# The causal mask of the first attention: fp32 mask products on TensorE, or an addition on VectorE with the row minimum

## The chip, the core and the metric

The kernel runs on one core of a Trainium2 chip. The metric is device time in microseconds (us): the median of several executions. The profile is of one execution, and its times are counted from the start of its span.

## What is computed

The program is two model blocks in a row. The first has 2 layers on 256 tokens of 1024 numbers, the second has 2 layers with a 32-expert layer each. The change touches the mixer of the first layer alone, an attention of 16 heads with keys of 64 + 32 numbers and values of 64:

```python
def mla_mixer(h, positions, w_a, q_norm, kv_norm, w_uq, w_ukv, w_o):
    ...
    q = (c_q @ w_uq).reshape(b, s_len, MLA_HEADS, MLA_NOPE + MLA_ROPE)
    q = jnp.concatenate([q[..., :MLA_NOPE], apply_rope(q[..., MLA_NOPE:], positions)], axis=-1)
    ...
    o = causal_block_attention(q, k, v, (MLA_NOPE + MLA_ROPE) ** -0.5)
    return o.reshape(b, s_len, MLA_HEADS * MLA_V) @ w_o

def causal_block_attention(q, k, v, scale, log_forget_cumsum=None):
    for b0 in range(0, s_len, Q_BLOCK):          # 256 tokens: two blocks of 128 queries
        b1 = b0 + Q_BLOCK
        logits = jnp.einsum('bqhd,bkhd->bhqk', q[:, b0:b1], k[:, :b1]).astype(jnp.float32) * scale
        causal = k_idx[None, :] <= q_idx[:, None]
        logits = jnp.where(causal, logits, NEG_INF)
        probs = jax.nn.softmax(logits, axis=-1).astype(v.dtype)
        outs.append(jnp.einsum('bhqk,bkhd->bqhd', probs, v[:, :b1]))
```

## The kernel before

Every engine has a program of its own, written out in order, and waits on semaphores. Nothing is scheduled by a planner: the order of the code is the order on the engine.

The attention is cut into 32 units, one for a head and a tile of 128 queries. Even units (tile 0) have 128 keys, odd units (tile 1) have 256; two units make a pair, one head. For unit u:

- PE, `scores(u)`: the fp32 product of queries and keys (line 924), then a second fp32 product, identity times the mask, added in the same bank (line 926). The trace has two MATMUL records for each fp32 product. Four banks hold the scores of four units, so that PE runs four units ahead.
- DVE, `row_max(u)`: the negative row maximum (TENSOR_REDUCE, line 2078), and its product with the scale 96^-0.5 (TENSOR_SCALAR on one column, line 2081).
- ACT: the exponential (line 1412) reads the bank, with the scale and that column as bias, writes the probabilities to SBUF and reads out their row sum (two records). `copy_probs(u)` (line 1403) copies the turned probabilities from PSUM to SBUF.
- PE, `turn_probs(u)`: one or two 128x128 transposes (line 951), which wait for the exponential; `values(u)`: one or two fp32 products of 64 columns (line 937), which wait for the copy. There are two banks for the turned probabilities and two for the outputs.
- DVE, `combine(u)`: the reciprocal of the row sum (line 2096), which waits for the exponential; `finish(u)`: the output divided by it, to `tokens_out` (line 2103).

In its loop over u, PE does scores(u+4), turn_probs(u), values(u-1); ACT does the exponential of u, then copy_probs(u-1); DVE does combine(u), row_max(u+4), finish(u-1). scores(u+4) waits until the exponential of u has read the bank. On DVE each instruction also waits for the end of the one before it (`v` in the code).

Ahead of the attention DVE copies the products of `g_uq` (the queries) out of PSUM, turns the last 32 numbers of each head by their angles, and PE transposes queries and keys (line 870). Behind it `close_block` transposes the output, splits it in two parts on DVE, and then lets POOL begin on the low parts of the weights (`port_free`). Weights come through a ring of four slots of 1 MB. When the first probabilities have been turned, POOL issues a transfer of 9 MB within DRAM (`rel_rows_repeated`, line 1766), which the second layer needs, and a row of gains (`broadcast_row`, line 1704), which the step behind the attention needs.

The same `attention` functions serve the second block's two-map attention (`kind="diff"`), which has no mask.

Of the kernel before, what the change touches and what calls it, by code (L numbers as in the profile page):

```python
# [11 lines left out]
ALU = mybir.AluOpType  # L12
# [3 lines left out]
P = 128  # L16
# [46 lines left out]
def constants():  # L63

    c = np.zeros((P, C_END), np.float32)
    i = np.arange(P)
    c[:, C_IDENT:C_IDENT + P] = np.eye(P)
    c[:, C_FLIP:C_FLIP + P] = np.eye(P)[::-1]
    col = np.arange(2 * P)
    c[:, C_CAUSAL:C_CAUSAL + 2 * P] = np.where(P + i[:, None] - col[None, :] >= 0, 0.0, NEG)  # L70
    qc = i % GRID_W
    start = np.clip(qc - NA_COLS // 2, 0, GRID_W - NA_COLS)
    kc = np.arange(GRID_W)
    ok = (kc[None] >= start[:, None]) & (kc[None] < start[:, None] + NA_COLS)
    c[:, C_NAMASK:C_NAMASK + GRID_W] = np.where(ok, 0.0, -NEG)
    c[:, C_UPPER:C_UPPER + P] = i[:, None] < i[None, :]
    half = 16
    inv = (np.float32(10000.0) ** (-np.arange(half, dtype=np.float32) / np.float32(half))).astype(np.float32)
    t = np.arange(SEQ)
    ar = (t // GRID_W).astype(np.float32)[:, None] * inv  # L80
    ac = (t % GRID_W).astype(np.float32)[:, None] * inv
    cos = np.cos(np.concatenate([ar, ar, ac, ac], 1)).astype(np.float32)
    sin = np.concatenate([-np.sin(ar), np.sin(ar), -np.sin(ac), np.sin(ac)], 1).astype(np.float32)
    for n in range(LT):
        c[:, C_COS + 64 * n:C_COS + 64 * n + 64] = cos[n * P:(n + 1) * P]
        c[:, C_SIN + 64 * n:C_SIN + 64 * n + 64] = sin[n * P:(n + 1) * P]
    c[:, C_INV:C_INV + half] = inv
    c[:, C_EIDX:C_EIDX + NE] = np.arange(NE)
    c[:, C_OIDX:C_OIDX + MAX_OVER] = np.arange(MAX_OVER)
    c[0, C_SEL:C_SEL + P] = 1.0  # L90
    c[1, C_SEL + P:C_SEL + 2 * P] = 1.0

    hot = np.zeros((64, DIL_G, BIAS_LEN), np.float32)
    exact = BUCKETS // 2
    for g, dil in enumerate(DILATION):
        for m in range(BIAS_LEN):
            dist = 2 * P - 1 - m
            if dist >= 0 and dist % dil == 0 and dist // dil <= SPAN:
                n = np.float32(max(dist, 1))
                large = exact + int(np.float32(np.log(n / np.float32(exact)) / np.float32(math.log(MAX_DIST / exact))  # L100
                                               * np.float32(BUCKETS - exact)))
                hot[dist if dist < exact else min(large, BUCKETS - 1), g, m] = 1.0
            else:
                hot[BUCKETS, g, m] = NEG
    return c, hot.reshape(64, DIL_G * BIAS_LEN)
# [31 lines left out]
def build_program(nc, I, out):  # L137
    ctx = ExitStack()
    with ctx:
# [281 lines left out]
            return ccol[:, c:c + 1]  # L421

        class Unit:
            def __init__(self, maps, n_keys, scale, values, width, dest, bias=None, kind="", head=0, tile=0):
                self.maps, self.n_keys, self.scale, self.values = maps, n_keys, scale, values
                self.width, self.dest, self.bias, self.kind, self.head, self.tile = width, dest, bias, kind, head, tile

        def mla_units():

# [4 lines left out]
            for h in range(MLA_H):  # L434
                for t in range(LT):
                    n = (t + 1) * P
                    maps = [[(0, n, qT[0:MLA_DK, h, t * P:(t + 1) * P], kT[0:MLA_DK, h, 0:n],
                              ident, causal[:, 2 * P - n:2 * P])]]
                    values = [kv[:, k, h, NOPE:NOPE + MLA_V] for k in range(t + 1)]
                    units.append(Unit(maps, n, MLA_DK ** -0.5, values, MLA_V,  # L440
                                      y_tile(t)[:, h * MLA_V:(h + 1) * MLA_V], head=h, tile=t))
            return place(units, True)

        N_PAIRS = DIL_H // 2
# [41 lines left out]
        def diff_units(layer):  # L486

            units = []
            for h in range(4):
                for t in range(all_tiles[layer]):  # L490
                    k0 = 0 if t < LT else LT * P
                    n = MAX_TILES * P - k0
                    maps = [[(m * BANK, n, qaT[64 * m:64 * m + 64, h, t * P:(t + 1) * P],
                              kaT[64 * m:64 * m + 64, h, k0:], None, None)] for m in range(2)]
                    values = [va[:, k, h, :] for k in range(k0 // P, MAX_TILES)]
                    units.append(Unit(maps, n, 1.0, values, P,
                                      ar(YA + t * 512, 512)[:, h * P:(h + 1) * P], kind="diff", head=h, tile=t))
            return place(units, False)

        def na_steps(layer):  # L500
# [197 lines left out]
        def _(pe):  # L698
# [212 lines left out]
            def attention(units):  # L911
# [5 lines left out]
                def scores(u):  # L917
                    unit = units[u]
                    if u >= n_held:
                        pe.wait_ge(exp_ready, base[s_ready.name] + u - n_held + 1)  # L920
                    for parts in unit.maps:
                        for col, n, q, k, turn, bias in parts:
                            dst = unit.scores[:, col:col + n]
                            last = nc.tensor.matmul(dst, q, k, start=True, stop=bias is None)
                            if bias is not None:
                                last = nc.tensor.matmul(dst, turn, bias, start=False, stop=True)
                    last.then_inc(s_ready, 1)
                    made.next(s_ready)

# [425 lines left out]
        def _(act):  # L1355
# [38 lines left out]
            def attention(units):  # L1394
# [10 lines left out]

                for u, unit in enumerate(units):
                    act.wait_ge(max_ready, base + u + 1)
                    if u >= held(units):
                        act.wait_ge(pT_ready, base + u - held(units) + 1)
                    for m in range(len(unit.maps)):  # L1410
                        c = stat(units, u, m)
                        last = nc.scalar.activation(unit.probs[:, m * BANK:m * BANK + unit.n_keys],
                                                    unit.scores[:, m * BANK:m * BANK + unit.n_keys], ACT.Exp,
                                                    bias=small[:, 64 + c:65 + c], scale=unit.scale,
                                                    accum_out=small[:, 80 + c:81 + c])
                    last.then_inc(exp_ready, 1)
                    if u >= 1:
# [512 lines left out]
        def _(dve):  # L1930
# [134 lines left out]
            def attention(units):  # L2065
                def row_max(u):
                    unit = units[u]
                    dve.wait_ge(s_ready, seen.next(s_ready))
                    if unit.kind == "diff":
# [1 line left out]
                        v(red(small[:, c:c + 2], unit.scores.rearrange("p (m k) -> p m k", m=2)[:, :, 0:unit.n_keys], X,  # L2071
                              ALU.max, negate=True), max_ready)
                        return
                    for m in range(len(unit.maps)):
                        c = 64 + stat(units, u, m)
                        last = m == len(unit.maps) - 1
                        scores = unit.scores[:, m * BANK:m * BANK + unit.n_keys]
                        v(red(small[:, c:c + 1], scores, X, ALU.max, negate=True),
                          max_ready if last and unit.scale == 1.0 else dve_step)
                        if unit.scale != 1.0:  # L2080
                            v(ts(small[:, c:c + 1], small[:, c:c + 1], unit.scale, None, ALU.mult), max_ready)

                def combine(u):

# [313 lines left out]
            for part in (c1, c2, c3):  # L2398
# [15 lines left out]
            norm_turn(LT, lambda t: ar(AROW + t * wide + MLA_QR, MLA_KVR),  # L2414
                      lambda g, t, n: XT[:, 2816:3328].rearrange("p (k t c) -> p k t c", k=2, t=LT)[:, 0:2, t, :],
                      2, gain=lambda t: V[:, V_KVN:V_KVN + 2])
            copy_product(g_uq, lambda n, t: ar(QROW + t * 1536 + n * BANK, BANK))

            for t in range(LT):
                sin = ang[:, t * 16:(t + 1) * 16]  # L2420
# [559 lines left out]
```

## Time and profile before

| | |
|---|---|
| median of 3 runs | 3340.39 us (3333.77 to 3341.43) |
| span of the profiled execution | 3333.3 us |
| PE busy | 2806.4 us (84%) |
| DVE busy | 1275.1 us (38%) |
| ACT busy | 877.4 us (26%) |
| POOL busy | 1089.3 us (33%) |
| attention of the first layer | 103.16 to 143.64 us, 40.5 us |

The page gives the profiled execution's span; what lies around it is not recorded, and the median of the runs is 7.1 us above this span. Busy shares are averages over stages that differ much: the two expert layers stream weights at up to 400 GB/s, while the stage of the change is small matrices on PE, DVE and ACT. So the stage is read by itself, 103 to 144 us. In a timeline row a start time, a duration, the engine, the line of the kernel, the operation, out<-in, and the count of merged instructions follow each other; in brackets stands the idle time before it and what ended it.

### The profile page before, as it was taken

The page shows a single profiled execution, that of the slowest core. Times are in us where ns is not written, and L with a number is a line of the kernel's source. Part 1 is how long each engine was busy: PE and PEld are TensorE (multiplying, and loading weights), DVE is VectorE, ACT ScalarE, POOL GpSimd, SP SyncE. Part 2 cuts the span into 40 slices and gives each one's busy share as a digit, 9 for nine tenths or more (in the row PEclk, how much of TensorE's full clock was granted, in tenths as well). Part 3 has the DMA queues.
Part 4 walks back from the last instruction along what each step waited for, and adds up shares of the span by engine and source line. Part 5 has one row for each costly group of instructions (what it writes and reads, how often), then busy time and mean ns, then how long its engine had stood idle before and what let it go on. Part 6 is the DMA issues. An engine that isn't in the chain of part 4 may idle for free.

```text
span 3333.3 us, 35642 instructions
## 1 busy us (share of the span) xinstructions
PE 2806.4 (84%) x13137; PEld 1834.4 (55%) x13137; DVE 1275.1 (38%) x2356; ACT 877.4 (26%) x1211; POOL 1089.3 (33%) x508
## 2 busy tenths in 40 slices
PE   6889879998998987889985988885797886988885
PEld 3767757777776775568762333332684772333331
DVE  4632144345225224753343322223427443322223
ACT  0433322235334212522221111112225331111111
POOL 0267746632874342224321000001363651000000
PEclk9989989999999998989987999998898997998998
DMA  5545488862554352622247999999241567999997
GB/s 159 171 150 176 158 296 291 288 223 70 166 173 152 139 164 98 216 89 91 101 152 277 390 401 399 399 398 357 76 139 49 179 234 289 391 396 397 396 398 288
DMA packets 218797, 781.17 MB, mean 234 GB/s; under 512 B 15092, under 2 KB 16290, under 8 KB 168752
## 3 DMA queue, kind: packets, MB, share of 16 engines
q1 hardware_dynamic: 189856, 669.61, 54.7%
q0 software_dynamic: 28816, 109.88, 9.9%
q8 instruction: 81, 1.33, 0.2%
q14 instruction: 44, 0.36, 0.0%
HBM read 750.36 MB, written 63.14 MB: 244 GB/s over the span
## 4 chain that ended last, share of the span: by engine, by line
PE 52%; DMA 22%; DVE 13%; SPq 6%; POOL 4%; ACT 2%; issue 2%; DVEq 0%; POOLq 0%; ACTq 0%
PE banks L737 11%; PE banks L738 10%; PE banks L742 10%; DMA weight_ring<-in_moe_w_down 4%; SPq L606 4%; PE banks L1131 4%; DMA arena<-in_moe_w_gate 3%; POOL weight_ring_r L1737 3%; DMA x_transposed<-in_moe_w_up 3%; DMA weight_ring<-in_moe_w_up 3%; DMA weights_high<-in_moe_w_gate 3%; PE banks L1154 2%; DMA tokens_out<-in_moe_w_down 2%; PE banks L820 2%; PE banks L870 2%
## 5 line engine op out<-in xcount | busy, mean ns | idle before, releaser
L1737 POOL TENSOR_TENSOR weight_ring_r<-weight_ring,weights_high_r 128x2048 fp32r<-128x2048 f32 x136 | 620.8, 4573 | 510.4 <-ACT weights_high_r L1387 419.8
L1387 ACT ACTIVATE weights_high_r<-weight_ring 128x2048 fp32r<-128x2048 f32 x136 | 257.5, 1901 | 736.4 <-PE banks L742 325.3
L737 PE MATMUL banks<-weights_high_r,x_transposed_r 128*128 128x512 f32 x1008 | 401.2, 398 | 33.9 <-ACT weights_high_r L1387 9.9
L1882 POOL DMA_DIRECT2D moe_y<-arena x64 | 33.9, 530 | 938.1 <-DVE arena L2570 922.1
L742 PE MATMUL banks<-weight_ring_r,x_transposed_r 128*128 128x512 f32 x1328 | 325.2, 391 | 2.1 <-POOL weight_ring_r L1737 2.1
L1737 POOL TENSOR_TENSOR weight_ring_r<-weight_ring,gates_r 128x2048 fp32r<-128x2048 f32 (+1 forms) x60 | 270.8, 4523 | 135.0 <-ACT gates_r L1387 73.8
L742 PEld LDWEIGHTS banks<-weight_ring_r,x_transposed_r 128*128 128x128 f32 x1328 | 249.5, 188 | 57.2 <-POOL weight_ring_r L1737 5.5
L737 PEld LDWEIGHTS banks<-weights_high_r,x_transposed_r 128*128 128x128 f32 x1008 | 192.6, 191 | 88.5 <-issue 26.4
L1593 ACT ACTIVATE arena<-banks 64x1024 f32<-64x1024 f32 x64 | 65.4, 1021 | 598.0 <-PE banks L1131 598.0
L738 PE MATMUL banks<-weights_high_r,arena_r 128*128 128x512 f32 x520 | 205.7, 396 | 0.0
L2552 DVE TENSOR_TENSOR arena<-banks,arena 64x1024 f32<-64x1024 f32 x64 | 77.9, 1217 | 312.9 <-ACT arena L1593 312.9
L1154 PE MATMUL banks<-weight_ring,arena 128*64 128x512 f32 x496 | 139.2, 703 | 35.5 <-DMA weight_ring<-in_moe_w_down 32.0
L2570 DVE TENSOR_TENSOR arena<-banks,arena 64x1024 f32<-64x1024 f32 x64 | 77.9, 1217 | 218.2 <-ACT arena L1607 218.2
L1101 PEld LDWEIGHTS banks<-constants,arena 64*128 64x128 f32 x256 | 69.6, 318 | 156.6 <-issue 155.0
L738 PE MATMUL banks<-weights_high_r,tokens_out_r 128*128 128x512 f32 x384 | 152.8, 398 | 0.0
L1387 ACT ACTIVATE gates_r<-weight_ring 128x2048 fp32r<-128x2048 f32 (+1 forms) x60 | 112.2, 1883 | 147.8 <-DMA weight_ring<-in_dil_w_qkv 87.9
L870 PE MATMUL banks<-constants,scaled_rows 128*128 128x128 f32 x482 | 80.4, 322 | 78.4 <-DVE scaled_rows L2008 67.1
L1131 PE MATMUL banks<-weight_ring,arena 128*64 128x512 f32 x528 | 126.2, 600 | 22.6 <-DMA weight_ring<-in_moe_w_up 12.0
L1131 PE MATMUL banks<-arena 128*64 128x512 f32 x512 | 123.1, 603 | 11.7 <-DMA arena<-in_moe_w_gate 11.7
L1101 PE MATMUL banks<-constants,arena 64*128 64x64 f32 x256 | 87.2, 421 | 54.0 <-DMA arena<-moe_x 54.0
L738 PE MATMUL banks<-weights_high_r,x_transposed_r 128*128 128x512 f32 x336 | 132.3, 394 | 0.0
L1607 ACT ACTIVATE arena<-banks 64x1024 f32<-64x1024 f32 x64 | 65.4, 1021 | 246.4 <-PE banks L1154 246.4
(383 smaller groups left out, 4886.3 us busy)
## 6 DMA issues: line engine op xcount, KB each, us to landing
weight_ring<-in_moe_w_down SPq DMA_DIRECT2D x62, 1024.0 KB, 30.6
weight_ring<-in_w_in SPq DMA_DIRECT2D x56, 1024.0 KB, 5.2
weight_ring<-in_w_ada SPq DMA_DIRECT2D x48, 1024.0 KB, 7.3
weight_ring<-in_ffn_w_in SPq DMA_DIRECT2D x44, 1024.0 KB, 5.1
weight_ring<-in_dil_w_qkv SPq DMA_DIRECT2D x36, 1024.0 KB, 5.2
tokens_out<-in_moe_w_gate SPq DMA_DIRECT2D x34, 1024.0 KB, 29.8
arena<-in_moe_w_up SPq DMA_DIRECT2D x34, 1024.0 KB, 29.2
weight_ring<-in_moe_w_up SPq DMA_DIRECT2D x34, 1024.0 KB, 28.9
```

Source lines behind the costliest of these rows:

```text
L606: sp.dma_start(slot(c, KG, BANK), src[e, half]).then_inc(w_in[slots[c]], 16)
L737: nc.tensor.matmul(banks[t][:, 0:width], xh, wh[:, k, :], start=k0 + k == 0, stop=False)
L738: nc.tensor.matmul(banks[t][:, 0:width], xl, wh[:, k, :], start=False, stop=False)
L742: last = nc.tensor.matmul(banks[t][:, 0:width], lhs(k0 + k, t)[0], wl[:, k, :], start=False, stop=k0 + k == g.k_tiles - 1)
L870: last = nc.tensor.transpose(bank[0:m, n * P:(n + 1) * P], src, ident)
L1101: return nc.tensor.matmul(dst, src, ident[0:CAP, 0:CAP], start=True, stop=True)
L1131: last = nc.tensor.matmul(halves(ps[m], kt), x, w[:, k, :], start=kt < 2, stop=kt >= KD - 2)
L1154: last = nc.tensor.matmul(halves(ps[2 + n], k), h, w[:, k % 2, n * BANK:(n + 1) * BANK], start=half == 0, stop=half == 1)
L1387: nc.scalar.activation(high(s, kn, width), slot(c, kn, width), ACT.Copy).then_inc(high_ready, 1)
L1737: nc.gpsimd.tensor_tensor(slot(c, kn, width, ring_r), slot(c, kn, width), high(s, kn, width), ALU.subtract).then_inc(low_ready, 1)
L2552: tt(A[0:CAP, E_SUM:E_SUM + 2 * BANK], pair[0][0:CAP, :], A[0:CAP, E_UP:E_UP + 2 * BANK], ALU.add).then_inc(summed, 1)
L2570: tt(A[0:CAP, E_Y + par * D:E_Y + (par + 1) * D], pair[1][0:CAP, :], A[0:CAP, E_YR:E_YR + D], ALU.add).then_inc(y_ready, 1)
```

## The change

The mask's products go. The scores alone are made on PE. DVE reads them and the mask in one instruction (`tensor_tensor_reduce`), writes their sum to the place of the probabilities in SBUF, and leaves the minimum of each row. To make the minimum serve, the queries are multiplied with -96^-0.5 when DVE takes them out of PSUM, and the mask has +1e30 in place of -1e30; the exponential is then taken of minus the sum. The one-column product with the scale goes too. The exponential reads SBUF and writes over what it read, so that PE's scores(u+4) waits for the row minimum of u and no longer for its exponential; in return the row minimum of u+4 waits until the probabilities of u have been turned, since it writes where they lie, and the exponential needs no such wait any more.

```diff
-    c[:, C_CAUSAL:C_CAUSAL + 2 * P] = np.where(P + i[:, None] - col[None, :] >= 0, 0.0, NEG)
+    c[:, C_CAUSAL:C_CAUSAL + 2 * P] = np.where(P + i[:, None] - col[None, :] >= 0, 0.0, -NEG)
...
                     if u >= n_held:
-                        pe.wait_ge(exp_ready, base[s_ready.name] + u - n_held + 1)
+                        pe.wait_ge(exp_ready if unit.mask is None else max_ready, base[s_ready.name] + u - n_held + 1)
                     for parts in unit.maps:
-                        for col, n, q, k, turn, bias in parts:
-                            dst = unit.scores[:, col:col + n]
-                            last = nc.tensor.matmul(dst, q, k, start=True, stop=bias is None)
-                            if bias is not None:
-                                last = nc.tensor.matmul(dst, turn, bias, start=False, stop=True)
+                        for col, n, q, k in parts:
+                            last = nc.tensor.matmul(unit.scores[:, col:col + n], q, k, start=True, stop=True)
...
                     act.wait_ge(max_ready, base + u + 1)
-                    if u >= held(units):
+                    if u >= held(units) and unit.mask is None:
                         act.wait_ge(pT_ready, base + u - held(units) + 1)
                     for m in range(len(unit.maps)):
                         c = stat(units, u, m)
-                        last = nc.scalar.activation(unit.probs[:, m * BANK:m * BANK + unit.n_keys],
-                                                    unit.scores[:, m * BANK:m * BANK + unit.n_keys], ACT.Exp,
-                                                    bias=small[:, 64 + c:65 + c], scale=unit.scale,
+                        probs = unit.probs[:, m * BANK:m * BANK + unit.n_keys]
+                        src = unit.scores[:, m * BANK:m * BANK + unit.n_keys] if unit.mask is None else probs
+                        last = nc.scalar.activation(probs, src, ACT.Exp, bias=small[:, 64 + c:65 + c],
+                                                    scale=1.0 if unit.mask is None else -1.0,
                                                     accum_out=small[:, 80 + c:81 + c])
...
-                    for m in range(len(unit.maps)):
-                        c = 64 + stat(units, u, m)
-                        last = m == len(unit.maps) - 1
-                        scores = unit.scores[:, m * BANK:m * BANK + unit.n_keys]
-                        v(red(small[:, c:c + 1], scores, X, ALU.max, negate=True),
-                          max_ready if last and unit.scale == 1.0 else dve_step)
-                        if unit.scale != 1.0:
-                            v(ts(small[:, c:c + 1], small[:, c:c + 1], unit.scale, None, ALU.mult), max_ready)
+                    if u >= held(units):
+                        dve.wait_ge(pT_ready, u - held(units) + 1)
+                    c, n = 64 + stat(units, u), unit.n_keys
+                    v(nc.vector.tensor_tensor_reduce(
+                        out=unit.probs[:, 0:n], in0=unit.scores[:, 0:n], in1=unit.mask, scale=1.0, scalar=3.0e38,
+                        op0=ALU.add, op1=ALU.min, accum_out=small[:, c:c + 1]), max_ready)
...
-            copy_product(g_uq, lambda n, t: ar(QROW + t * 1536 + n * BANK, BANK))
+            for n in range(len(g_uq.chunks)):
+                for t in range(LT):
+                    bank = product_bank()
+                    v(ts(ar(QROW + t * 1536 + n * BANK, BANK), bank[:, :], -MLA_DK ** -0.5, None, ALU.mult), acc_used)
```

PE in the loop of the attention, before: two units, from a value product of one to that of the next but one (scores_ready is `s_ready` in the code, probsT_ready `pT_ready`, probsT_copied `pTs_ready`, attn_out_used `o_used`).

```order
L937 MATMUL banks6<-arena,x_transposed 128x64
L924 MATMUL banks2<-arena 128x256 [waits exp_ready]
L926 MATMUL banks2<-constants 128x256
L951 MATMUL banks4<-constants,tokens_out 128x128 [waits probsT_copied,exp_ready]
L951 MATMUL banks4<-constants,tokens_out 128x128
L937 MATMUL banks6<-arena,x_transposed 128x64 [waits attn_out_used,probsT_copied]
L924 MATMUL banks0<-arena 128x128 [waits exp_ready]
L926 MATMUL banks0<-constants 128x128
```

PE at the same place after.

```order
L932 MATMUL banks6<-arena,x_transposed 128x64
L921 MATMUL banks2<-arena 128x256 [waits max_ready]
L946 MATMUL banks4<-constants,tokens_out 128x128 [waits probsT_copied,exp_ready]
L946 MATMUL banks4<-constants,tokens_out 128x128
L932 MATMUL banks6<-arena,x_transposed 128x64 [waits attn_out_used,probsT_copied]
L921 MATMUL banks0<-arena 128x128 [waits max_ready]
```

Each unit loses its second product, and the scores wait for DVE's row minimum; the order of the rest stands.

DVE in the same loop, before.

```order
L2096 RECIPROCAL small<-small 128x1 [waits exp_ready,attn_out_used]
L2078 TENSOR_REDUCE small<-banks2 128x1 [waits scores_ready,vector_step]
L2081 TENSOR_SCALAR small<-small 128x1 [waits vector_step]
L2103 TENSOR_SCALAR tokens_out<-banks6,small 128x64 [waits attn_out_ready,max_ready]
L2096 RECIPROCAL small<-small 128x1 [waits exp_ready,attn_out_used]
```

DVE after (ISA is the `tensor_tensor_reduce`, and behind it the read of its accumulator).

```order
L2090 RECIPROCAL small<-small 128x1 [waits exp_ready,attn_out_used]
L2073 ISA tokens_out,small<-banks2,constants 128x128 [waits probsT_ready,scores_ready,vector_step]
L2073 ISA small 128x1
L2097 TENSOR_SCALAR tokens_out<-banks6,small 128x64 [waits attn_out_ready,max_ready]
L2090 RECIPROCAL small<-small 128x1 [waits exp_ready,attn_out_used]
```

The row minimum has one more wait, for the transposes of the unit four before it, and stands between the reciprocal and the output of its neighbours as the row maximum did.

## Rows read from the trace of the kernel before

**Rows 1.** Windows of the attention: engines' busy time (instructions), granted clock, DMA.

```profile
103.00:107.50 4.50, 4.34 (x16) 3.80 (x17) 1.48 (x7) 2.20 (x5) 0.00 (x0) 0.62 0.00 0
...
125.00:130.00 5.00, 5.00 (x39) 4.61 (x38) 4.06 (x18) 2.81 (x12) 0.00 (x0) 1.00 1.04 338
```

**Rows 2.** Groups by line and form, 101.5 to 142 us: busy us, mean ns.

```profile
L926 PE MATMUL banks<-constants 128*128 128x256 f32 x32 | 10.3, 405 | 0.0
```

**Rows 3.** Timeline of PE, one pair of units.

```profile
127.83 0.44 PE L924 MATMUL banks<-arena 96*128 96x128 f32 x2
128.11 0.39 PE L926 MATMUL banks<-constants 128*128 128x128 f32 x2
128.33 0.27 PE L951 MATMUL banks<-constants,tokens_out 128*128 128x128 f32 x1
...
129.32 0.60 PE L926 MATMUL banks<-constants 128*128 128x256 f32 x2
129.76 0.38 PE L951 MATMUL banks<-constants,tokens_out 128*128 128x128 f32 x2
...
130.15 0.44 PE L924 MATMUL banks<-arena 96*128 96x128 f32 x2
```

**Rows 4.** Timeline of DVE, the same pair.

```profile
127.72 0.42 DVE L2078 TENSOR_REDUCE small<-banks 128x1 f32<-128x256 f32 x1 [0.15 <-PE banks L926]
128.17 0.15 DVE L2081 TENSOR_SCALAR small<-small 128x1 f32<-128x1 f32 x1
...
128.68 0.16 DVE L2096 RECIPROCAL small<-small 128x1 f32<-128x1 f32 x1
128.88 0.29 DVE L2078 TENSOR_REDUCE small<-banks 128x1 f32<-128x128 f32 x1
129.20 0.15 DVE L2081 TENSOR_SCALAR small<-small 128x1 f32<-128x1 f32 x1
```

**Rows 5.** Timeline of ACT, the same pair.

```profile
130.18 0.38 ACT L1403 ACTIVATE x_transposed<-banks 128x256 f32<-128x256 f32 x1 [0.91 <-PE banks L951]
```

**Rows 6.** Timeline of DVE in the second layer's attention: tensor_tensor_reduce and its neighbours.

```profile
712.94 0.56 DVE L2181 CUSTOM_DVE_ANT_1 gates<-banks,tokens_out 128x384 f32<-128x384 f32 x1
...
713.54 0.56 DVE L2181 CUSTOM_DVE_ANT_1 gates<-banks,tokens_out 128x384 f32<-128x384 f32 x1
...
750.72 0.42 DVE L2191 COPY x_transposed<-banks 128x256 f32<-128x256 f32 x1
751.18 0.96 DVE L2181 CUSTOM_DVE_ANT_0 gates<-banks,tokens_out 128x768 f32<-128x768 f32 x1
```

**Rows 7.** Timeline of the attention's start.

```profile
103.16 0.46 PE L924 MATMUL banks<-arena 96*128 96x128 f32 x2 [2.33 <-DVE arena L1991]
...
103.95 0.29 DVE L2078 TENSOR_REDUCE small<-banks 128x1 f32<-128x128 f32 x1 [0.94 <-PE banks L926]
...
104.52 1.28 ACT L1412 ACT_TABLE_LOAD   x1 [56.65 <-DVE small L2081]
...
105.81 0.37 ACT L1412 ACTIVATE tokens_out<-banks,small 128x128 f32<-128x128 f32 x1
...
106.08 0.19 ACT L1412 ACTIVATION_READ_ACCUMULATOR tokens_out<-banks,small 128x1 f32 x1
...
108.91 0.29 DVE L2078 TENSOR_REDUCE small<-banks 128x1 f32<-128x128 f32 x1 [0.30 <-DVE small L2096]
```

**Rows 8.** Timeline of DVE: the last row maximum and the last output.

```profile
139.27 0.42 DVE L2078 TENSOR_REDUCE small<-banks 128x1 f32<-128x256 f32 x1
...
143.36 0.28 DVE L2103 TENSOR_SCALAR tokens_out<-banks,small 128x64 f32<-128x64 f32 x1 [0.57 <-PE banks L937]
```

**Rows 9.** Waits, 142 to 260 us: in total, times, longest.

```profile
POOL weight_ring_r L1737 <- DVE small L1947: 39.0, 1, 39.0
```

**Rows 10.** DMA issues, 80 to 150 us: KB each, median us to landing.

```profile
rel_rows_repeated<-rel_rows POOLq DMA_DIRECT2D x1, 9216.0 KB, 35.2
```

**Rows 11.** Window of the second block's two-map attention, columns as in rows 1.

```profile
1360.00:1375.00 15.00, 12.89 (x75) 7.61 (x74) 13.82 (x35) 9.79 (x29) 0.00 (x0) 1.00 1.01 317
```

More of the change, by code:

```diff
@@ L423, in build_program, with __init__ @@
         class Unit:
-            def __init__(self, maps, n_keys, scale, values, width, dest, bias=None, kind="", head=0, tile=0):
-                self.maps, self.n_keys, self.scale, self.values = maps, n_keys, scale, values
-                self.width, self.dest, self.bias, self.kind, self.head, self.tile = width, dest, bias, kind, head, tile
+            def __init__(self, maps, n_keys, values, width, dest, mask=None, kind=""):
+                self.maps, self.n_keys, self.values = maps, n_keys, values
+                self.width, self.dest, self.mask, self.kind = width, dest, mask, kind
         def mla_units():
@@ L436, in mla_units @@
                     n = (t + 1) * P
-                    maps = [[(0, n, qT[0:MLA_DK, h, t * P:(t + 1) * P], kT[0:MLA_DK, h, 0:n],
-                              ident, causal[:, 2 * P - n:2 * P])]]
+                    maps = [[(0, n, qT[0:MLA_DK, h, t * P:(t + 1) * P], kT[0:MLA_DK, h, 0:n])]]
                     values = [kv[:, k, h, NOPE:NOPE + MLA_V] for k in range(t + 1)]
-                    units.append(Unit(maps, n, MLA_DK ** -0.5, values, MLA_V,
-                                      y_tile(t)[:, h * MLA_V:(h + 1) * MLA_V], head=h, tile=t))
+                    units.append(Unit(maps, n, values, MLA_V, y_tile(t)[:, h * MLA_V:(h + 1) * MLA_V],
+                                      mask=causal[:, 2 * P - n:2 * P]))
             return place(units, True)
@@ L493, in diff_units @@
                     maps = [[(m * BANK, n, qaT[64 * m:64 * m + 64, h, t * P:(t + 1) * P],
-                              kaT[64 * m:64 * m + 64, h, k0:], None, None)] for m in range(2)]
+                              kaT[64 * m:64 * m + 64, h, k0:])] for m in range(2)]
                     values = [va[:, k, h, :] for k in range(k0 // P, MAX_TILES)]
-                    units.append(Unit(maps, n, 1.0, values, P,
-                                      ar(YA + t * 512, 512)[:, h * P:(h + 1) * P], kind="diff", head=h, tile=t))
+                    units.append(Unit(maps, n, values, P, ar(YA + t * 512, 512)[:, h * P:(h + 1) * P], kind="diff"))
             return place(units, False)
```

## The prediction

> **What bounds the kernel now.** I read the page first, then the windows around the changed stage, the groups by line in it, and one pair of units on each engine in the timeline. The page's averages say little about a stage of 40 us in 3333. The window from 125 us has PE busy for all of its 5.00 us at the full clock (1.00), DVE for 4.06, ACT for 3.01 or less [rows 1]. So PE looks like the bound, but the starts have to be read too, because a PE record overlaps the next one, and a DVE instruction waits for the one before it.
>
> By starts on PE, a pair takes 130.15 - 127.83 = 2.32 us. In it the mask product of 128 columns holds PE from 128.11 to 128.33, 0.22 us, and that of 256 columns from 129.32 to 129.76, 0.44 us [rows 3]. No gap stands before them.
>
> By starts on DVE, the same pair needs: row maxima 0.45 (127.72 to 128.17) and 0.32 (128.88 to 129.20); one scale product and one output 0.51 (128.17 to 128.68), twice 1.02; one reciprocal 0.20 (128.68 to 128.88), twice 0.40. The sum is 2.19 us [rows 4]. So DVE is only 0.13 us per pair behind PE, and the first row of the group even shows where it waits 0.15 us for a mask product. ACT sits idle for 0.91 us of each pair, waiting for transposes [rows 5]. The reader should see two engines close together: taking work from PE alone is worth 0.13 us a pair, and the rest depends on what DVE loses.
>
> **What PE loses.** 32 mask products, of both widths in equal number; the wider ones' records are busy 10.3 us with overlaps [rows 2]. By starts it is 0.22 + 0.44 = 0.66 us a pair, and PE would need 2.32 - 0.66 = 1.66.
>
> **What DVE gains and loses.** The second layer has this very instruction, with a PSUM and an SBUF input and its accumulator read behind it: 128x384 takes 713.54 - 712.94 = 0.60 us from start to start [rows 6]. The row maxima tell the price of 128 more columns, 0.45 - 0.32 = 0.13 [rows 4]. So 256 columns cost 0.47 and 128 columns 0.34, together 0.81 against 0.77 for the row maxima: 0.04 more. The scale product costs 0.19, which is its 0.15 and the 0.04 that lie between any two DVE instructions, twice a pair: 0.38 less. DVE needs 2.19 + 0.04 - 0.38 = 1.85 us a pair. The third wait in front of the row minimum costs nothing where it is already met: an instruction of this kind with more waits starts 0.46 us after a copy of 0.42 [rows 6], the usual 0.04.
>
> **Edits at nothing.** The scale in the queries' copy replaces a DVE copy out of PSUM of the same size by a one-input DVE instruction of the same size, six times; if it were slower by a tenth of a copy, the whole would be under 0.5 us. ACT reads SBUF in place of PSUM, also at the same size; a tenth of a microsecond more for each of two exponentials a pair would disappear in the 0.91 us. If ACT had no such cover, it would be 3 us over the stage. PE's new wait, for the row minimum of the unit four before, is met earlier than the exponential that it replaces.
>
> **The loop.** DVE at 1.85 becomes the bound, with PE at 1.66 and ACT at 2.32 - 0.91 = 1.41. From the loop's first row maximum at 108.91 to the last at 139.27 [rows 7, 8] there are 27 units, 13.5 pairs, in 30.36 us, 2.25 a pair: nearly DVE's 2.19 while PE's lead of four units lasts, then PE's 2.32. After the change: 13.5 x 1.85 = 25.0 us. This saves 5.4 us.
>
> **The start.** PE begins at 103.16 after 2.33 us idle [rows 7], and the window from 103.0 has a clock of 0.62 [rows 1]: by that mean it is at 1.2 GHz in place of 2.4 for some 3.4 us, which I put from 103.7 to 107.1 (an estimate). The first DVE row waits for the first mask product, and ACT loads its table behind DVE's scale product. Without the mask product (0.22) and the scale product (0.19) the table load starts about 0.4 earlier, at 104.1, ends at 105.4, and the first exponential with the read of its sum is done 0.46 us later, at about 105.9 [rows 7]. Meanwhile PE has to make five score products; at half clock 128 columns take 0.44 and 256 columns 0.88, three and two of them are 3.1 us less 0.5 for the first ones at full clock, so it is done at about 105.8. The first transposes come at about 106.0, and the loop's first row minimum at about 106.5 instead of 108.91: 2.4 us. From there to 107.1 PE is at half clock and needs 3.32 a pair against DVE's 1.85; of 0.6 us about 0.3 is lost. Net 2.1. Its bounds are 0 (the exponential comes no earlier, if the clock comes back later for the missing products) and 2.4.
>
> **The end.** From the last row maximum to the last output it takes 4.09 us [rows 8] of transposes, copies and value products, and none of it changes.
>
> **The sum.** 5.4 + 2.1 = 7.5 us. It reaches the end of the kernel: POOL's low parts wait for DVE behind the attention, 39.0 us in one piece [rows 9], and everything behind follows in a chain. Nothing of the later stages is changed. The profiled span of 3333.3 becomes 3325.8; with the 7.1 us by which the median of the runs lies above the span I predict 3332.9 us, a ratio of 0.9978.
>
> **The rivals.**
>
> *PE stays the bound.* If DVE's accumulator read ran beside the next instruction, DVE would be below PE's 1.66; the loop would save 30.36 - 13.5 x 1.66 = 7.9 and the whole 10.0: 3330.4. Against it stands the even spacing of 0.60 in rows 6, where the next instruction waits for the end of the read.
>
> *The new wait takes the gain.* On DVE the reciprocal, the row minimum and the output stand in one line. If PE is not ahead, the row minimum of u+4 waits for the transposes of u, which PE issues only after scores(u+4); the output of u-1 stands behind it, and PE's value product two units on waits for that. With one transposes' record (0.27 [rows 3]) exposed in each unit the pair costs 1.85 + 0.54 = 2.39, so the loop takes 32.3, 1.9 more than now, which the start's 2.1 pays: 3340.2. For it: the wait is real and in every unit from the fifth. Against it: PE needs 0.19 less a pair than DVE, so it should hold its lead; between the ends I would expect under 0.1 a pair, 1.3 us.
>
> *Slower: PE's clock falls.* Once PE has gaps, its clock may go to 1.2 GHz in the middle of the attention. A pair then costs 2 x 1.66 = 3.32, the loop 44.8, that is 14.4 more less 2.1 at the start: 3352.7. It decides from the share of the loop at half clock: each pair there costs 3.32 - 1.85 = 1.47 more than forecast, and the whole gain of 7.5 us is gone after 5.1 of the 13.5 pairs. The window of the second block's attention speaks against it: PE busy 12.89 of 15.00 us, with gaps and transposes as here, and the clock at 1.00 [rows 11]. After the change PE would be busy 1.66 of 1.85, a higher share.
>
> The Trainium skill (TensorE: Matmul & The Clock Gate, "Part 4: PE-mode transpose") says that transposes do not count as busy for the clock as products do, and in "A second HAM failure mode: psum-queue depth-cycling" that small idles between groups of products can make the clock swing. By these the clock falls in the loop and this rival's time holds; by rows 11 it does not, and the trace goes against the rule as far as it shows.
>
> *Given back.* The 9 MB transfer issued at the first transposes takes 35.2 us [rows 10], now nearly as long as the attention. If the chain behind the attention needed its bandwidth, the end would move by the start's 2.1 us only, or not at all: 3340.4. The first weights behind the attention are in the ring already, so I see nothing that needs it.
>
> **Chances.** Forecast 0.64, PE the bound 0.13, new wait 0.12, clock falls 0.05, given back 0.06. What a measurement of this kernel can tell from no change is about 0.3%, 10.0 us. The forecast of 7.5 has its own spread of some 3 us, from the start and from where the clock's dips fall in the other stages (the runs before lie 7.7 us apart): from 3330 to 3337, with a fourth of it beyond 10.0. Faster: 0.64/4 + half of 0.13 + a little = 0.24. Slower: 0.05 + 0.02 from the given-back case = 0.07. The same: 0.69. The range for 8 in 10 takes in PE as the bound with its spread, and the cases without a gain: 3326 to 3342.
>
> **What the profile after would show.** Of the forecast: DVE's row minima 0.34 and 0.47 us from start to start to the next; a pair every 1.85 us on DVE with no idle; small idle times on PE; about 33 us from the first score product to the last output instead of 40.5; the clock at 1.00 from 108 us. Of the rivals: pairs of 1.66; DVE idle before the row minimum, ended by transposes; a clock under 1.00 in the windows after 108; or POOL's first low part behind the attention not about 7 us earlier. The forecast is wrong if the pair is over 2.0 us or the attention shrinks by less than 5 us, and its sum is right in the wrong place if the later stages move by more than 3.

## The result, and the profile after

The changed kernel takes 3351.11 us (median of 20 executions, 3330.11 to 3362.95), the kernel before 3338.11 in the same comparison (20 executions, 3330.78 to 3348.58). The ratio is 1.003, 95% interval 1.0018 to 1.0043: slower by a little, where I had forecast 0.9978. The medians lie 13.0 us apart. The time lies outside the range of 3326 to 3342, on the side that had a chance of 0.07, and 1.6 us from what the rival *Slower: PE's clock falls* gave, 3352.7.

The page of the profiled execution has these lines; PE's busy time is up by 5.0 us although the 64 records of the mask products are gone.

```profile
span 3343.6 us, 35486 instructions
PE 2811.4 (84%) x13073; PEld 1842.4 (55%) x13073; DVE 1278.1 (38%) x2356; ACT 878.9 (26%) x1211; POOL 1090.0 (33%) x508
```

The windows, in the columns of [rows 1], the first two for the same stretches:

```profile
103.00:107.50 4.50, 3.68 (x13) 3.01 (x14) 2.19 (x10) 2.71 (x7) 0.00 (x0) 0.65 0.00 0
125.00:130.00 5.00, 5.00 (x21) 4.50 (x20) 2.77 (x14) 2.39 (x11) 0.00 (x0) 0.50 1.01 329
...
150.00:155.00 5.00, 4.85 (x23) 4.19 (x23) 2.51 (x11) 3.43 (x12) 0.00 (x0) 0.50 0.00 0
155.00:160.00 5.00, 4.38 (x23) 4.10 (x23) 2.97 (x7) 5.00 (x4) 0.00 (x0) 0.60 0.00 0
160.00:165.00 5.00, 5.00 (x24) 4.12 (x23) 3.02 (x6) 3.04 (x3) 1.69 (x1) 1.00 0.01 3
```

PE is busy for 5.00 of 5.00 us from 125, as it was before, and the reader could stop there. But the count beside it has fallen from 39 matmul records to 21, where only 4 of a pair's 17 records are gone, and the granted clock from 1.00 to 0.50: 1.2 GHz in place of 2.4. It stays there in every window from 107.5 to 155 us and comes back only behind the attention. A busy share does not tell a full engine from a slow one; the count and the clock do.

PE's timeline, one pair, to set beside [rows 3]:

```profile
127.61 0.74 PE L921 MATMUL banks<-arena 96*128 96x128 f32 x2
128.15 0.42 PE L946 MATMUL banks<-constants,tokens_out 128*128 128x128 f32 x1
128.36 0.95 PE L932 MATMUL banks<-arena,x_transposed 128*128 128x64 f32 x4
129.11 1.17 PE L921 MATMUL banks<-arena 96*128 96x256 f32 x2
130.07 0.63 PE L946 MATMUL banks<-constants,tokens_out 128*128 128x128 f32 x2
130.49 0.53 PE L932 MATMUL banks<-arena,x_transposed 128*128 128x64 f32 x2
130.81 0.53 PE L921 MATMUL banks<-arena 96*128 96x128 f32 x1
```

A pair takes 130.81 - 127.61 = 3.20 us, with no idle. DVE's timeline of the same pair, beside [rows 4]:

```profile
127.68 0.43 DVE L2073 CUSTOM_DVE_ANT_0 tokens_out<-banks,constants 128x256 f32<-128x256 f32 x1 [0.97 <-PE banks L946]
128.03 0.08 DVE L2073 DVE_READ_ACCUMULATOR2_ANT small<- 128x1 f32 x1
128.15 0.29 DVE L2097 TENSOR_SCALAR tokens_out<-banks,small 128x64 f32<-128x64 f32 x1
```

The row minimum of 256 columns costs 128.15 - 127.68 = 0.47 from start to start, exactly the forecast, but DVE stands idle before it for 0.97 us until PE has made the transposes. Over the attention its waits say the same (in total, times, longest):

```profile
ACT x_transposed L1398 <- PE banks L946: 23.0, 28, 1.5
DVE tokens_out L2073 <- PE banks L946: 13.6, 15, 1.0
```

The window is 103 to 153 us. The wait on transposes is the new one that the rival *The new wait takes the gain* spoke of, yet it is no cause: PE has no idle in the pair above, so the transposes are late because PE is slow. The start and the end, in the timelines of PE, DVE, ACT and POOL:

```profile
103.72 2.73 PE L921 MATMUL banks<-arena 96*128 96x128 f32 x10 [2.33 <-DVE arena L1987]
...
106.00 0.40 ACT L1409 ACTIVATE tokens_out<-tokens_out,small 128x128 f32<-128x128 f32 x1
...
106.55 0.48 PE L946 MATMUL banks<-constants,tokens_out 128*128 128x128 f32 x1
...
107.58 0.29 DVE L2073 CUSTOM_DVE_ANT_0 tokens_out<-banks,constants 128x128 f32<-128x128 f32 x1 [0.79 <-PE banks L946]
...
155.62 0.28 DVE L2097 TENSOR_SCALAR tokens_out<-banks,small 128x64 f32<-128x64 f32 x1 [0.98 <-PE banks L932]
...
163.31 4.58 POOL L1733 TENSOR_TENSOR weight_ring_r<-weight_ring,weights_high_r 128x2048 fp32r<-128x2048 f32 x1 [52.97 <-DVE small L1943]
```

From the first score product to the start of the last output, "the attention" below, it takes 155.62 - 103.72 = 51.9 us. Before it was 143.36 - 103.16 = 40.2 [rows 7, 8]. So 11.7 us are lost here, and the whole span is 10.3 longer. POOL's first low part begins 12.7 us later (163.31 for 150.58), where the forecast had it 7 earlier.

### The profile page after: what moved, and what is told of

Same layout as the page of the kernel before. It is cut to its first block, busy times and chain, and to the rows that moved or that the text cites. A ratio compares the mean times of both kernels' runs of the same rounds, so it can differ in the third digit from the quotient of the medians.

```text
span 3343.6 us, 35486 instructions
## 1 busy us (share of the span) xinstructions
PE 2811.4 (84%) x13073; PEld 1842.4 (55%) x13073; DVE 1278.1 (38%) x2356; ACT 878.9 (26%) x1211; POOL 1090.0 (33%) x508
## 4 chain that ended last, share of the span: by engine, by line
PE 52%; DMA 20%; DVE 12%; SPq 6%; POOL 4%; ACT 3%; issue 2%; DVEq 0%; POOLq 0%; ACTq 0%
PE banks L735 11%; PE banks L736 10%; PE banks L740 10%; DMA weight_ring<-in_moe_w_down 4%; SPq L604 4%; PE banks L1126 4%; POOL weight_ring_r L1733 3%; DMA arena<-in_moe_w_gate 3%; DMA weight_ring<-in_moe_w_up 3%; DMA x_transposed<-in_moe_w_up 3%; PE banks L1149 2%; DMA tokens_out<-in_moe_w_down 2%; PE banks L818 2%; DMA weights_high<-in_moe_w_gate 2%; SPq L612 2%
```

## The experiments

My theory after the result: in both kernels the granted clock falls to 0.50 (1.2 GHz) just after PE's idle time, 0.79 us behind the start of the first score product before and 0.64 behind it after (by half-us windows). Before, the mask products make the opening dense enough for the clock to rise; the changed kernel has half the products there, and goes at once into a loop in which it never rises. The rivals: the clock would also fall from 2.4 GHz in such a loop, whatever the opening (so the change can't be saved); the transposes, not the missing products, hold it down; or DVE and its waits are the cause. All edits are to the changed kernel, except two to the kernel before. A discarded product writes to a bank that a later product starts anew.

**Mask products back, for all units or for the first eight.**

```diff
 for col, n, q, k in parts:
+    if unit.mask is not None and True:       # second kernel: and u < 8
+        nc.tensor.matmul(unit.scores[:, col:col + n], ident, unit.mask, start=True, stop=True)
     last = nc.tensor.matmul(unit.scores[:, col:col + n], q, k, start=True, stop=True)
```

> The changed kernel, and before each masked score product PE makes the mask product as well, in the same bank, where the score product overwrites it. PE has the work of the kernel before, all else is as changed. Theory D (density: without the mask products PE's activity in the loop is too low for the full clock, wherever it starts): clock 1.00 in the loop, pair 2.3 us, attention about 39 us instead of 52, time 3335 to 3341. Theory S (start: the dense products of the first microseconds raise the clock, and the loop would hold it by itself): the same here. Rival W (the new wait or the DVE instruction makes the loop slow, the clock only follows): the attention stays at 50 us or more, time about 3351.

Measured: 3342.6 us, ratio 1.0009 (0.9999 to 1.0019), attention 40.0 us, clock back at 1.00 from 108.1. With PE's old work the loss goes, and the gain with it: DVE's new instruction and all new waits are in this kernel, so they are not what costs 11.7 us.

> As the run with discarded mask products, but for the first 8 units alone; units 8 to 31 have the changed loop. Theory S: the clock rises by about 108 us and stays at 1.00, the loop then runs at about 1.85 a pair, attention about 34 us, time 3331 to 3335. Theory D: the clock rises, then falls to 0.50 after the eighth unit and the rest runs at 3.2 a pair; attention about 45 us or more, time 3344 to 3350.

Measured: 3338.06 us, ratio 0.9999 (0.9987 to 1.0011), attention 34.3 us. Its windows:

```profile
103.00:107.50 4.50, 3.85 (x14) 3.34 (x15) 1.54 (x7) 2.34 (x5) 0.00 (x0) 0.64 0.00 0
107.50:115.00 7.50, 7.50 (x54) 6.72 (x52) 5.08 (x26) 4.48 (x20) 2.69 (x2) 0.99 0.35 130
...
125.00:130.00 5.00, 5.00 (x38) 4.31 (x37) 4.43 (x22) 4.09 (x18) 0.00 (x0) 1.00 1.02 321
```

The clock falls at the start as in the changed kernel, rises at 107.7 and stays up through a loop that is, from unit 8, instruction for instruction that of the changed kernel, with 38 records in 5 us in place of 21. The loop does not lower the clock. This speaks against the first rival.

**Work in the idle time ahead.** Five discarded products, or twenty discarded transposes, in the 2.33 us before the first scores.

```diff
 pe.wait_ge(acc_used, ...)
+if units[0].mask is not None:
+    for _ in range(5):                       # other kernel: 20 transposes of 128 columns
+        nc.tensor.matmul(ps[3][:, 0:2 * P], ident, causal, start=True, stop=True)
 pe.wait_ge(tr_used, ...)
```

> The changed kernel with five more discarded products (identity times mask, 256 columns) in PE's 2.3 us of idle before the first scores. Theory S: the clock does not fall at 103.7 or comes back at once, loop at 1.85 a pair, attention about 32 us, time 3329 to 3333. Theory D: the clock falls in the loop whatever stands before it, 3.2 a pair in most of it, time 3345 to 3352.

Measured: 3334.3 us, ratio 0.999 (0.9977 to 1.0004), attention 31.8 us. The windows of five products:

```profile
100.00:103.00 3.00, 2.85 (x17) 2.40 (x17) 2.83 (x6) 0.00 (x0) 0.00 (x0) 1.00 0.00 0
103.00:107.50 4.50, 3.36 (x20) 2.49 (x18) 2.33 (x11) 2.77 (x8) 0.01 (x1) 1.00 0.00 0
...
120.00:125.00 5.00, 5.00 (x38) 4.32 (x37) 4.44 (x23) 3.73 (x17) 0.00 (x0) 1.00 0.98 308
```

and its DVE timeline, one pair:

```profile
128.13 0.42 DVE L2076 CUSTOM_DVE_ANT_0 tokens_out<-banks,constants 128x256 f32<-128x256 f32 x1
...
129.11 0.29 DVE L2076 CUSTOM_DVE_ANT_0 tokens_out<-banks,constants 128x128 f32<-128x128 f32 x1
129.33 0.08 DVE L2076 DVE_READ_ACCUMULATOR2_ANT small<- 128x1 f32 x1
129.45 0.28 DVE L2100 TENSOR_SCALAR tokens_out<-banks,small 128x64 f32<-128x64 f32 x1
...
129.96 0.42 DVE L2076 CUSTOM_DVE_ANT_0 tokens_out<-banks,constants 128x256 f32<-128x256 f32 x1
```

The clock never leaves 1.00, and a pair takes 129.96 - 128.13 = 1.83 us on a DVE without idle: 1.85 was forecast.

> The changed kernel with 20 discarded transposes of 128 columns in PE's 2.3 us of idle before the first scores, about as long as the five discarded products of 256 columns of the run before. Theory T (transposes count little for the clock): the clock falls at about 103.7 as in the changed kernel and stays at 0.50, attention about 52 us, time 3345 to 3352. Theory B (PE only has to be busy, with whatever): the clock stays at 1.00, attention about 32 us, time 3330 to 3336.

Measured: 3336.14 us, ratio 0.9975 (0.9961 to 0.9988), attention 31.8 us. The windows of twenty transposes:

```profile
100.00:103.00 3.00, 2.94 (x26) 2.71 (x25) 2.35 (x4) 0.00 (x0) 0.00 (x0) 1.00 0.00 0
103.00:107.50 4.50, 3.44 (x23) 2.89 (x23) 2.76 (x15) 3.94 (x13) 1.17 (x1) 1.00 0.01 2
```

Transposes keep the clock up here as products do.

> The changed kernel with the five discarded products in the idle stretch ahead of the attention, as before, once more. The attention was 31.8 us in one profile; the time was 0.1% under before, with an interval that reaches from -0.23% to +0.04%. If the full clock holds in every run, the ratio is 0.9975, 8 us, as the attention's 8.4 us say; if part of it is given back behind the attention, it stays at 0.999.

Measured: 3335.69 us, ratio 0.9979 (0.9968 to 0.999), attention 31.8 us, clock at 1.00 throughout. This is the five products again, beside the unaltered change on the same chip (below).

**Transposes as products.** In the loop, the probabilities are turned by fp32 products with the identity.

```diff
-                        last = nc.tensor.transpose(turned_probs(units, u)[:, k * P:(k + 1) * P],
-                                                   unit.probs[:, k * P:(k + 1) * P], ident)
+                        turn = nc.tensor.transpose if unit.mask is None else (
+                            lambda o, a, b: nc.tensor.matmul(o, a, b, start=True, stop=True))
+                        last = turn(turned_probs(units, u)[:, k * P:(k + 1) * P],
+                                    unit.probs[:, k * P:(k + 1) * P], ident)
```

> The changed kernel with the transposes of the probabilities in this attention made as fp32 products with the identity (two records in place of one, and about 0.21 us in place of 0.11 for 128 columns at full clock). Theory D with transposes that count little for the clock: clock 1.00 in most of the loop, although PE's work by time is 2.0 to 2.6 a pair; attention 36 to 43 us, time 3333 to 3342. If transposes count as much as products: the clock stays at 0.50, PE has more to do at half clock, over 4 a pair, attention 60 us or more, time 3360 or more.

Measured: 3343.2 us, ratio 1.0016 (1.0006 to 1.0027), attention 37.6 us. Its windows:

```profile
103.00:107.50 4.50, 4.50 (x17) 3.86 (x16) 2.09 (x12) 2.92 (x8) 0.69 (x1) 0.50 0.01 2
107.50:115.00 7.50, 7.50 (x53) 7.34 (x53) 4.88 (x24) 4.44 (x19) 2.01 (x2) 0.86 0.70 240
...
125.00:130.00 5.00, 5.00 (x42) 4.90 (x41) 3.83 (x20) 3.46 (x14) 0.00 (x0) 1.00 0.99 316
```

With nothing else changed, the clock comes back at 109.6, 7.1 us behind the first score product (102.49), while the loop runs. One profile is weak, since the unaltered change can raise its clock too (below). But none of the 12 executions took over 3352.03 us, where I had expected 3360 or more if the clock stayed low under this heavier work. Products in place of transposes can raise it. Whether it is their kind or their number (an fp32 product has two records, a transpose one), this kernel doesn't tell apart.

**The kernel before, with the same edits.**

> The kernel before with five discarded products in the same idle stretch. If the full clock at the start is all that they give, the attention shrinks by the 2 us or so that the half clock cost there, 40.2 to about 38, and the time by 1 to 2 us, to about 3337. If most of the gain of the changed kernel with five such products was theirs alone, the time falls by 4 us or more here too.

Measured: 3344.57 us against 3343.62, ratio 0.9998 (0.9984 to 1.0013), attention 39.1 us: the clock, held up from the start, is worth 1.1 us in this stage before, and 20.1 after (51.9 to 31.8).

The next one takes the one-column product away alone, and puts the scale into the copies of the queries, without the minus sign:

```diff
-units.append(Unit(maps, n, MLA_DK ** -0.5, values, MLA_V,
+units.append(Unit(maps, n, 1.0, values, MLA_V,
...
-            copy_product(g_uq, lambda n, t: ar(QROW + t * 1536 + n * BANK, BANK))
+            for n in range(len(g_uq.chunks)):
+                for t in range(LT):
+                    bank = product_bank()
+                    v(ts(ar(QROW + t * 1536 + n * BANK, BANK), bank[:, :], MLA_DK ** -0.5, None, ALU.mult), acc_used)
```

> The kernel before with the scale in the queries and without the one-column product; the mask products stay on PE. My step: PE is the bound at 2.32 us a pair, so DVE's 0.38 less a pair is worth only the few pairs in which DVE was the bound (2.19): attention 40.2 to 39 or 40 us, pairs still 2.31, time within 1 us of before. Rival: DVE was the bound after all, and a pair falls to 2.0: attention 36 us, time 4 us less.

Measured: 3345.22 us, ratio 1.001 (0.9997 to 1.0023), attention 40.2 us as before. DVE's timeline:

```profile
127.93 0.16 DVE L2096 RECIPROCAL small<-small 128x1 f32<-128x1 f32 x1
128.52 0.42 DVE L2078 TENSOR_REDUCE small<-banks 128x1 f32<-128x256 f32 x1 [0.43 <-PE banks L926]
```

What DVE saves, it waits for the mask product: PE was the bound, and the scaled copies cost nothing to be seen.

**The change, unaltered, twice more.**

> The changed kernel, unaltered, one more execution with a profile. Its 20 timed runs had three at 3330 to 3333 and the rest at 3343 to 3363. If the clock's rise in the attention is a matter of chance from run to run, this profile shows either an attention of about 52 us at 0.50, or one of 32 to 36 us at 1.00; anything between (40 us) would say that the clock can also rise inside the loop.

Measured, one execution: 3333.94 us, attention 32.2 us. Its windows:

```profile
103.00:107.50 4.50, 4.50 (x21) 3.73 (x20) 2.29 (x13) 3.37 (x10) 0.66 (x1) 0.62 0.01 2
107.50:115.00 7.50, 7.50 (x54) 6.48 (x54) 6.66 (x33) 5.81 (x25) 2.03 (x2) 1.00 0.70 240
...
125.00:130.00 5.00, 5.00 (x38) 4.30 (x36) 4.44 (x23) 3.73 (x17) 0.00 (x0) 1.00 1.01 308
```

The same instructions and the same fall of the clock at the start, and here it rises again, at 106.4; all of the forecast follows. Windows of half a us show both edges, and a difference. First the fall in the slow execution of the result, then the fall and the rise in this one:

```profile
104.00:104.50 0.50, 0.50 (x4) 0.41 (x3) 0.18 (x1) 0.00 (x0) 0.00 (x0) 0.85 0.00 0
...
102.50:103.00 0.50, 0.22 (x2) 0.25 (x3) 0.14 (x1) 0.00 (x0) 0.00 (x0) 0.98 0.00 0
...
106.00:106.50 0.50, 0.50 (x3) 0.42 (x3) 0.24 (x3) 0.43 (x4) 0.00 (x0) 0.61 0.00 0
```

From the means, the clock fell at 104.36 in the slow one, 0.64 us behind its first score product (103.72), and at 102.98 in this one, 0.20 behind it (102.78).

> The changed kernel unaltered, in the same rounds as the two others. If the clock stays at 0.50 in most of its runs, the median is 8 to 13 us above before, with single runs 15 to 20 us below the others; and it is 12 to 18 us above the kernel with five discarded products, whose work per unit is the same.

Measured: 3353.42 us, ratio 1.0021 (1.0004 to 1.0037), attention 51.9 us, clock at 0.50 in every window of it. In the 31 executions of the change in all, five took 3329.04 to 3333.94 us, and 26 took 3343.10 to 3362.95, with none between. On the same chip the five discarded products (3335.69) are 17.7 us below, near the 20.1 that the attention differs by.

**Raised in the middle.** Eight discarded products before the scores of unit 16.

```diff
 if unit.mask is not None and u == 16:
+    for _ in range(8):
+        nc.tensor.matmul(unit.scores[:, 0:2 * P], ident, causal, start=True, stop=True)
```

> The changed kernel with eight discarded products of 256 columns in one place, before the scores of unit 16. Theory H (the changed loop cannot raise the clock but holds it once raised): where the profile has the clock at 0.50 up to unit 16, it is back at 1.00 within some microseconds of the eight products and stays there to the attention's end; pairs 3.2 us before and 1.85 behind; attention about 52 - 8 x 1.35 + 4 = 44 us, time about 3343. Rival (the loop holds neither): it falls back to 0.50 behind them, attention about 56 us, time 3352 or more. If the clock happens to be at 1.00 from the start, the products cost up to 3.5 us and the attention is about 35 us; then the profile decides nothing.

Measured: 3349.45 us, ratio 1.0019 (1.0004 to 1.0033). Undecided: in the profiled execution (3342.95 us, attention 35.5) the clock had come up by 108 already. So I ran it three times more, one execution each.

> As the run with eight discarded products at unit 16, once more. If the clock is at 0.50 up to them: by theory H it is at 1.00 within some microseconds of them and stays there to the end of the attention, pairs 3.2 us before and 1.85 behind, attention about 44 us; by the rival it falls back to 0.50 within 10 us, attention about 56 us.

> The same kernel and the same expectation as the run before; it counts where its clock is at 0.50 when the eight products come.

> The same kernel and the same expectation as the run before; it counts where its clock is at 0.50 when the eight products come.

Measured: 3349.44, 3343.62 and 3354.97 us; attentions 44.8, 44.6 and 44.7. In all three the clock is at 0.50 until the eight products, rises 3.8 to 4.1 us into them, and is at 1.00 from there to the end of the loop. PE's timeline of the third:

```profile
117.82 0.74 PE L924 MATMUL banks<-arena 96*128 96x128 f32 x2
...
121.02 0.74 PE L924 MATMUL banks<-arena 96*128 96x128 f32 x2
...
124.22 5.60 PE L921 MATMUL banks<-constants 128*128 128x256 f32 x16
...
133.10 0.44 PE L924 MATMUL banks<-arena 96*128 96x128 f32 x2
...
134.94 0.44 PE L924 MATMUL banks<-arena 96*128 96x128 f32 x2
```

and its windows:

```profile
120.00:125.00 5.00, 5.00 (x21) 4.42 (x20) 2.42 (x12) 2.39 (x9) 0.00 (x0) 0.50 0.98 315
125.00:130.00 5.00, 5.00 (x19) 4.13 (x19) 0.20 (x2) 0.01 (x1) 0.00 (x0) 0.69 1.01 321
130.00:135.00 5.00, 5.00 (x39) 4.39 (x38) 3.93 (x20) 3.52 (x16) 0.00 (x0) 1.00 1.00 306
```

One execution, one loop, and two paces: 3.20 us a pair before the eight products (121.02 - 117.82), 1.84 behind them (134.94 - 133.10). Behind the rise the loop keeps the clock that it was given. This decides against the first rival within a single execution.

Together: of seven profiled executions with the changed kernel's instructions up to unit 15, two raised the clock at the start by themselves and five did not; of the four with mask products there and the clock low at first (before, both refills, the scaled copy), all had it up by about 108.

So few profiles could mislead, but the times without one say the same. Over 3343 us were 26 of the 31 executions of the unaltered change, 2 of the 11 with mask products for eight units, and 2 of the 34 with work in the idle time.

**The version that beats both** is the change with work in PE's idle time ahead: 0.9975 with transposes, 0.9979 and 0.999 with products. It takes 8.4 us off the attention; the medians fall by 7.5, 7.2 and 4.4 us. In two of the three comparisons the interval excludes 1, in the third (0.9977 to 1.0004) it does not.

## Why the prediction was wrong

- *What bounds the kernel now*: right. PE bound the loop before, DVE close behind; saving on DVE alone is worth nothing (scaled copy).
- *What DVE gains and loses*, *What PE loses*, *Edits at nothing*: right. Row minimum 0.47, pair 1.83 to 1.84 against 1.85, but only at 2.4 GHz. At 1.2 GHz I had reckoned 3.32 for a pair, and it is 3.20.
- *The loop*: right given the clock. With the clock up the attention takes 31.8 to 32.2 us; 40.2 - 7.5 = 32.7 was forecast.
- ***The start*: here it failed.** "From there to 107.1 PE is at half clock": I took the moment at which the clock came back before and kept it for a kernel with half the products in front of it. I even wrote that the clock may come back "later for the missing products", and priced that at a gain of 0, not at what follows if it doesn't come back at all: 13.5 pairs at 3.20 in place of 1.85, 18 us. The rest of the step held: this attention began 0.56 later than before (103.72), the first transposes came 0.55 later than I had put them (106.55 for 106.0), the loop's first row minimum at 107.58 for 106.5. But the clock never rose: 0.50 in every window from 107.5 to 155, and an attention of 51.9 us.
- *Slower: PE's clock falls*: the price was right (3352.7; 3351.11 measured), the mechanism only in part. PE has no gaps in the slow loop and nothing falls there; the clock falls at the start, as before, and fails to come back. It is in part luck that the median landed 1.6 us from this rival's time, which had 3.32 us for a pair and the start's gain with it. My argument against it was faulty: [rows 11] show a stage in which the clock is up already. They show that gaps and transposes do not lower it (true here too: both refills and all gap kernels), and I read them as if they showed that it rises.
- The Trainium skill (TensorE: Matmul & The Clock Gate, "Part 4: PE-mode transpose") has transposes not counting as busy for the clock in the way that products do. The runs go against it where the clock is to be held (twenty transposes did it), and do not go against it where it is to be raised (at half clock, products in their place raised it, by their kind or their number). What the Trainium skill says in the same page's section "A second HAM failure mode: psum-queue depth-cycling", a clock that swings with small idles between groups of products, did not show: PE is busy for 5.00 of 5.00 us in each window of the slow loop from 115 to 150, and the clock stays at 0.50.
- *The new wait* and *Given back*: not seen. With the clock up, DVE has no idle in the loop, and 7 to 8 us of the 8.4 reach the end in two comparisons of three. Why it was 4.4 in the third is not settled; its interval reaches from 7.7 gained to 1.3 lost.
- *The sum*: five of 31 executions lie at 3329 to 3334, around the 3332.9 of the forecast. Which clock each execution without a profile had, I can't tell.

What stays open: why the loop, once at 1.2 GHz, doesn't raise the clock, and what makes the start of one execution raise it where another's doesn't. One thing goes with it in the seven profiles with the changed kernel's start: in the two that raised the clock it had fallen 0.17 and 0.20 us behind the first score product, in the five that did not 0.61 to 0.90 us. No edit moved that moment alone, so it is not shown to be the cause. The four kernels with mask products had it fall 0.60 to 0.79 us behind their first product and raised it all the same, which speaks for the missing products and not for the moment alone. And the first expert product came 15.1 us later than before (1804.8 for 1789.7), where the span ended 10.3 longer; what made up the rest was not tried.

## What to carry to other kernels

Taking work from PE behind an idle time can cost more than the work: ask of each stage not only whether its clock is up, but which products raised it, and whether enough of them remain. A row from a stage that is at full clock shows that such work keeps it, not that it brings it. A few discarded products or transposes in the idle time ahead (2.3 us of them here) cost nothing that could be measured (0.9998 on the kernel before) and are worth trying wherever a stage of short instructions starts low; and read the count and the granted clock beside PE's busy time.

## What the runs showed of the hardware

- This loop of short products and transposes kept either clock: 1.2 GHz from 107.5 to 155 us with hardly a gap in PE's records, or 2.4 GHz after a raise (3.20 and 1.84 us a pair in one execution).
- Behind the 2.33 us of idle the clock fell in all twelve profiles that had this idle, 0.17 to 0.90 us after PE's first product behind the idle; in the four in which the idle was filled it did not fall.
- 5.6 us of dense fp32 products raised it in three executions of three (the fourth had it up already).
- Twenty transposes in the idle time kept it at 1.00 as ten records of products did.
- The rise behind this idle time differs between executions of the changed kernel, and its times fall in two groups, 3329 to 3334 and 3343 to 3363 us. The one profile from the lower group has the rise, the two from the upper do not.
- A mask product (identity times mask) of 128 fp32 columns held PE for 0.22 us and one of 256 for 0.44 at 2.4 GHz [rows 3]; a DVE `tensor_tensor_reduce` with its accumulator read took 0.34 and 0.47 from start to start for the same widths.
